# An encoder layer on one core: tokens in residue order, bias tables as one Toeplitz block per residue distance

## The chip, the cores and the metric

The kernel runs on one core of one Trainium2 chip. The metric is the device time of one execution in microseconds (us). TensorE is written PE, VectorE DVE, ScalarE ACT, GpSimd POOL, SyncE SP.

## What is computed

One encoder layer over two sequences, a prompt of 512 tokens and a sample of 256, model width 1024, all in float32. After an RMSNorm, one projection gives the queries, keys, values and gates of two attention branches: differential attention (4 heads, all keys) and dilated attention (3 groups of 4 heads). Their gated sum is projected back, and a mixture of 16 expert MLPs follows. A T5 table adds to each logit a bias that depends only on key position minus query position. The dilated branch, cut to what matters:

```python
DIL_CONFIGS = ((128, 1), (512, 4), (2048, 16))     # (window, dilation)
def dilated_group(q, k, v, bias_table, window, dilation):
    # Query i attends to i + m*dilation for |m*dilation| <= window/2 (keys gathered by stride).
    L = S // dilation
    def residues(t):
        return t.reshape(B, L, dilation, H, dh).transpose(0, 2, 1, 3, 4)
    ...
    off = jnp.arange(KW)[None, :] - W - jnp.arange(Q_BLOCK)[:, None]
    band = jnp.abs(off) <= W
    bias = bias_table[t5_bucket(off * dilation)].transpose(2, 0, 1)
    s = jnp.einsum('bmnqhd,bmnkhd->bmnhqk', qr, kblk) * scale + bias
    s = jnp.where(mask, s, NEG_INF)
    ...
# alpha = softmax of the three groups' log-denominators; ob = sum(alpha * outs)
```

## The kernel before

The 768 tokens are 6 tiles of 128: 4 of the prompt (`TP`), 2 of the sample. `ht_hi` and `ht_lo` hold the normed tokens turned round (model dimension on partitions, tokens in their order along the row), split in two float32r parts, so that each float32 product is three matmuls (`passes`, lines 777 to 779).

PE's order is written out by hand. It goes through 46 *halves* (`HALVES`), each a 128-column or 3-tile piece of the projection, and in fixed *slots* beside them it does the attention: one *unit* is (branch, head, tile), and `SCORES_IN` puts two units into a slot. In a slot PE turns the probabilities of the two units before (L835), forms the scores of two new ones (L815 differential, L823 and L825 dilated), does the half, and then multiplies probabilities by values (L857). A head's six units are its four prompt tiles and then its two sample tiles. Halves 0 to 3 are the differential values, 4 to 11 differential queries and keys, 12 to 17 the dilated values (two halves for each group g = 0, 1, 2), 18 to 29 the dilated queries and keys, 30 to 45 the gates. Differential scores stand in slots 9 to 20, dilated ones in slots 26 to 37.

Dilated attention needs the tokens of one residue (mod 4 in the prompt, mod 2 in the sample). `tile_columns` and `query_columns` pick them out of token order with a step: every 4th float32 column for prompt tiles, every 2nd for sample tiles. Three matmuls use this. The dilated values of groups 1 and 2 (halves 14 to 17) read `ht_hi` and `ht_lo` so as the stationary operand. Dilated scores read the queries so as the stationary operand; in the two far groups (L825) they read the keys so too, as the moving operand. One half's three tiles are 3 x 24 matmuls; the first half of a group holds prompt tiles 0 to 2, the second prompt tile 3 and both sample tiles.

The bias tables are made at the start: a one-hot matmul (`vectors`, L769, in slots 1 to 3) expands the table into vectors of length `VEC` = 3072 for 16 heads, ACT copies them out (`copy_vectors`) and stores them to DRAM, and POOL's `load_bias` reads skewed rows of them back. There are 8 loads, one per head and branch, into two buffers (`n % 2`). A load waits on `s_max` until every unit of the load two before it has been through `add_bias` on DVE (L1380 differential, L1388 and L1389 dilated).

Of the kernel before, what the change touches and what calls it, by code (L numbers as in the profile page):

```python
# [24 lines left out]
F32 = mybir.dt.float32  # L25
# [7 lines left out]
P = 128  # L33
# [26 lines left out]
SEC_DIFF, SEC_NEAR, SEC_D4, SEC_D16, SEC_SAMPLE_D4, SEC_SAMPLE_D16 = 0, 1024, 2048, 2304, 2560, 2816  # L60
# [93 lines left out]
VEC_SLOTS = 1  # L154
SUB_SLOT = {22: [0, 1], 23: [2, 3]}
# [27 lines left out]
BIAS_DMAS = [1] * H + [6] * H  # L183
# [18 lines left out]
def build(nc, x_prompt, x_sample, rel_bias, norm_mix, w_in, lam_q1, lam_k1, lam_q2, lam_k2, subln_g,  # L202
# [9 lines left out]
    with ctx:  # L212
# [31 lines left out]
        BIAS_W = 516 + 256 + 258 + 258  # L244
# [24 lines left out]
        junk = at("junk", [P, D], F32, A_ATT + 28800)  # L269
# [168 lines left out]

        def rows_of(t):
            return (x_prompt[0, P * t:P * t + P, :] if t < TP  # L440
                    else x_sample[0, P * (t - TP):P * (t - TP) + P, :])

        def out_rows(t):
            return (y_prompt[0, P * t:P * t + P, :] if t < TP
                    else y_sample[0, P * (t - TP):P * (t - TP) + P, :])
# [167 lines left out]
        def _(gp):  # L613
# [7 lines left out]
            def load_bias(n):  # L621

                if n >= 2:

                    gp.wait_ge(s_max, NT * (n - 1))
                b = bias[:, n % 2, :]
                done = s_bias[n % 2]
                if n < H:  # L630
                    gp.dma_start(b[:, 0:896], bass.AP(vec, n * VEC + SEC_DIFF, [[1, P], [1, 896]])).then_inc(done, 16)
                    return
                h = n - H
                r0 = (4 + h) * VEC + SEC_NEAR
                r1 = (8 + h) * VEC + SEC_D4
                r2 = (12 + h) * VEC + SEC_D16
                r3 = (8 + h) * VEC + SEC_SAMPLE_D4
                r4 = (12 + h) * VEC + SEC_SAMPLE_D16
                gp.dma_start(b[:, 0:516], bass.AP(vec, r0, [[4, P], [1, 516]])).then_inc(done, 16)
                gp.dma_start(b[:, 772:1029], bass.AP(vec, r0 + 256, [[2, P], [1, 257]])).then_inc(done, 16)  # L640
                for at0, r in ((516, r1), (516 + P, r2), (1030, r3), (1030 + P, r4)):
                    gp.dma_start(b[:, at0:at0 + P], bass.AP(vec, r, [[1, P], [1, P]])).then_inc(done, 16)

            gp.wait_ge(s_vec_out, 16)
            for n in range(2 * H):
                load_bias(n)
# [79 lines left out]
        def _(pe):  # L726
# [55 lines left out]
            def half(s):  # L782
                c, j = divmod(s, 2)
                if j == 0:
                    pe.wait_ge(s_wlo, c + 1)
                kind = HALVES[s][0]
                ps = main_item("half", s)
                hi, lo = e8(w_hi[:, c % 2, :]), e8(w_lo[:, c % 2, :])
                if kind in ("q", "k", "gate"):
                    cols = slice(P * j, P * j + P)  # L790
                    for a, b in ((0, 512), (512, T)):
                        last = passes(ps[:, a:b], [((hi[:, k, cols], lo[:, k, cols]),
                                                    (ht_hi[:, k, a:b], ht_lo[:, k, a:b])) for k in range(KD)])
                else:
                    res = kind == "vl" and HALVES[s][1] > 0
                    for i in range(3):
                        t = 3 * j + i
                        if s < 2:
                            pe.wait_ge(s_work_v, t + 1)
                        last = passes(ps[:, 256 * i:256 * i + 256],  # L800
                                      [((tile_columns(ht_hi[:, k, :], t, res), tile_columns(ht_lo[:, k, :], t, res)),
                                        (hi[:, k, :], lo[:, k, :])) for k in range(KD)])
                        if s < 2 and t + 2 < NT:
                            turn_x(t + 2)
                last.then_inc(s_main, 1)

            def score(u):
# [3 lines left out]
                if not dil:  # L811
                    for c in range(2):
                        rows = slice(HD * c, HD * c + HD)
                        at0 = c * 512
                        last = pe.matmul(ps[:, at0:at0 + S], query_columns(blk[rows, DIFF_Q[h], :], t, False),  # L815
                                         blk[rows, DIFF_K[h], s0:s0 + S], start=True, stop=True)
                else:
                    rows = slice(HD * (h % 2), HD * (h % 2) + HD)
                    for g in range(N_DIL):
                        q = query_columns(blk[rows, DIL_Q[h // 2][g], :], t, True)  # L820
                        k = blk[rows, DIL_K[h // 2][g], :]
                        if g == 0:
                            last = pe.matmul(ps[:, 0:S], q, k[:, s0:s0 + S], start=True, stop=True)  # L823
                        else:
                            last = pe.matmul(ps[:, 384 + P * g:512 + P * g], q, tile_columns(k, t, True),  # L825
                                             start=True, stop=True)
# [43 lines left out]
            for s in range(N_SLOTS):  # L870
# [8 lines left out]
                if VEC_SLOTS <= s < VEC_SLOTS + 3:  # L879
# [175 lines left out]
        def _(act):  # L1055
# [36 lines left out]
            def copy_vectors(i):  # L1092
                ps = work_ready("vec", i)
                act.activation(vecs[:, 1024 * i:1024 * i + 1024], ps[0:16, :], ACT.Copy).then_inc(s_work_a, 1)
                if i == 2:

                    act.wait_ge(s_work_a, emptied(WORK, WORK_NO[("vec", 2)], WORK_BY_VECTOR)[1])
# [25 lines left out]
            def empty_pv(u):  # L1123
# [6 lines left out]
                act.activation(tile_columns(ob[rows, h // 2, :], t, True)[:, ::-1], ps[rows, 0:P], ACT.Copy).then_inc(s_work_a, 1)  # L1130
# [19 lines left out]
            for s in range(N_SLOTS):  # L1150
# [9 lines left out]
                if VEC_SLOTS <= s < VEC_SLOTS + 3:  # L1160
                    copy_vectors(s - VEC_SLOTS)
                if s == VEC_SLOTS + 3:
# [158 lines left out]
        def _(dve):  # L1321
# [44 lines left out]
            def add_bias(u):  # L1366

                dil, h, t = UNITS[u]
                n = H * dil + h
                _, S = sequence(t)  # L1370
# [3 lines left out]
                if t == 0:  # L1374
                    dve.wait_ge(s_bias[n % 2], bias_count(n))
                dve.wait_ge(s_work, WORK_NO[("score", u)] + 1)
                if not dil:
                    at0 = 384 - P * (t if t < TP else t - TP)
                    for c in range(2):
                        last = dve.tensor_tensor_reduce(prob[:, i, 512 * c:512 * c + S], ps[:, 512 * c:512 * c + S],  # L1380
                                                        b[:, at0:at0 + S], 1.0, LOWEST, ALU.add, ALU.max, mx[:, i, c:c + 1])
# [4 lines left out]
                near = b[:, 3 - t:3 - t + S] if t < TP else b[:, 773 - (t - TP):773 - (t - TP) + S]  # L1386
                far = b[:, 516:772] if t < TP else b[:, 1030:1286]
# [32 lines left out]
            for s in range(N_SLOTS):  # L1420
# [6 lines left out]
                if s == VEC_SLOTS + 4:  # L1427
# [305 lines left out]
def _onehot(np):  # L1733
# [8 lines left out]
    rel = np.arange(-511, 513)  # L1742
    put(SEC_DIFF, rel, rel > 511)
    put(SEC_NEAR, rel, np.abs(rel) > 64)
# [35 lines left out]
```

## Time and profile before

| | us |
|---|---|
| median of 3 runs | 1008.6 |
| lowest, highest | 1008.04, 1009.04 |
| profiled execution, span from first to last instruction | 1006.1 |
| PE busy | 894.9 (89%) |
| DVE busy | 470.4 (47%) |
| ACT busy | 395.8 (39%) |
| POOL busy | 186.7 (19%) |

Of the profiled execution the span is shown, 2.5 us under the median of the runs. Busy shares are means over stages with different limits. Matmuls overlap their neighbours, so the start of one matmul to the start of the next tells what it costs, and its own duration does not.

### The profile page before, as it was taken

What the parts mean: (1) busy time and instruction counts of PE and PEld (TensorE: products, weight loads), DVE (VectorE), ACT (ScalarE), POOL (GpSimd) and SP (SyncE); (2) the same over time, 40 slices, a digit from 0 to 9 for tenths busy, and PEclk for the clock granted to TensorE, in tenths of its full rate; (3) what the DMA queues carried; (4) which work ended last, traced back from release to release, by engine and by line L of the source; (5) the groups of instructions that cost most, each with busy time, mean ns of one, the idle gap of its engine ahead of it and who ended that gap; (6) DMA issues with size and microseconds to landing.
All of it is one profiled execution on the core that took longest, in us unless ns stands there. A gap on an engine that the chain in (4) does not pass through costs nothing.

```text
span 1006.1 us, 13215 instructions
## 1 busy us (share of the span) xinstructions
PE 894.9 (89%) x5004; PEld 768.8 (76%) x5004; DVE 470.4 (47%) x754; ACT 395.8 (39%) x534; POOL 186.7 (19%) x124
## 2 busy tenths in 40 slices
PE   4999999999999999999999999999814999899920
PEld 4988788998788888888888888888613788788810
DVE  4411544333519523132322126622484688768638
ACT  5432444233433433324333211211530677677614
POOL 0000000001010010100000000400051476768644
PEclk9999999999999998999999999999955999999975
DMA  9231210112130321111102121691692699998775
GB/s 295 74 97 43 84 52 18 54 42 52 26 94 8 84 69 42 27 42 43 43 19 66 43 83 43 208 401 48 252 333 70 216 386 379 377 330 299 239 273 228
DMA packets 96397, 140.41 MB, mean 140 GB/s; under 512 B 4283, under 2 KB 75147, under 8 KB 96299
## 3 DMA queue, kind: packets, MB, share of 16 engines
q1 hardware_dynamic: 89276, 114.91, 33.8%
q0 software_dynamic: 7040, 24.61, 7.6%
q8 instruction: 35, 0.57, 0.2%
q10 hardware_dynamic: 32, 0.20, 0.2%
q14 instruction: 14, 0.11, 0.0%
HBM read 114.34 MB, written 25.36 MB: 139 GB/s over the span
## 4 chain that ended last, share of the span: by engine, by line
PE 78%; DVE 9%; DMA 4%; ACT 4%; issue 2%; SPq 2%; POOL 1%; ACTq 0%; POOLq 0%; DVEq 0%
PE main L777 20%; PE main L778 20%; PE main L779 20%; PE work L857 4%; PE work L823 2%; PE work L815 2%; PE work L825 2%; PE work L997 2%; DMA xg<-h_rows,column 1%; PE work L835 1%; ACT prob_t L1121 1%; DVE x L1715 1%; DMA e_raw<-in_w_exp_down 1%; DVE w_lo L1332 1%; PE work L950 1%
## 5 line engine op out<-in xcount | busy, mean ns | idle before, releaser
L777 PE MATMUL main<-ht_hi,w_hi 128*128 128x512 f32 (+1 forms) x576 | 198.5, 345 | 0.0
L778 PE MATMUL main<-ht_lo,w_hi 128*128 128x512 f32 (+1 forms) x576 | 195.6, 340 | 0.0
L779 PE MATMUL main<-ht_hi,w_lo 128*128 128x512 f32 (+1 forms) x576 | 195.2, 339 | 0.0
L1332 DVE TENSOR_TENSOR w_lo<-raw,w_hi 128x2048 fp32r<-128x2048 f32 x30 | 68.7, 2290 | 265.7 <-ACT w_hi L1065 265.7
L777 PEld LDWEIGHTS main<-ht_hi,w_hi 128*128 128x128 f32 x576 | 110.3, 192 | 19.0 <-issue 6.4
L779 PEld LDWEIGHTS main<-ht_hi,w_lo 128*128 128x128 f32 x576 | 110.2, 191 | 12.2
L778 PEld LDWEIGHTS main<-ht_lo,w_hi 128*128 128x128 f32 x576 | 110.4, 192 | 11.9
L777 PE MATMUL main<-w_hi,ht_hi 128*128 128x256 f32 (+1 forms) x304 | 102.4, 337 | 3.4 <-DVE ht_lo L1349 3.4
L778 PE MATMUL main<-w_lo,ht_hi 128*128 128x256 f32 (+1 forms) x304 | 100.8, 332 | 0.0
L779 PE MATMUL main<-w_hi,ht_lo 128*128 128x256 f32 (+1 forms) x304 | 100.7, 331 | 0.0
L1213 ACT ACTIVATE e_hi<-e_raw 128x2048 fp32r<-128x2048 f32 x48 | 90.5, 1910 | 15.2 <-DMA e_raw<-in_w_exp_down 6.8
L1511 DVE TENSOR_TENSOR e_lo<-e_raw,e_hi 128x2048 fp32r<-128x2048 f32 x31 | 71.5, 2337 | 21.4 <-ACT e_hi L1213 21.3
L777 PEld LDWEIGHTS main<-w_hi,ht_hi 128*128 128x128 f32 x304 | 67.8, 223 | 11.7 <-issue 8.5
L778 PEld LDWEIGHTS main<-w_lo,ht_hi 128*128 128x128 f32 x304 | 67.9, 223 | 2.5
L779 PEld LDWEIGHTS main<-w_hi,ht_lo 128*128 128x128 f32 x304 | 67.8, 223 | 2.5
L1065 ACT ACTIVATE w_hi<-raw 128x2048 fp32r<-128x2048 f32 x30 | 57.2, 1907 | 25.9 <-PE main L779 24.3
L685 POOL TENSOR_TENSOR e_lo<-e_raw,e_hi 128x2048 fp32r<-128x2048 f32 x13 | 61.6, 4740 | 25.5 <-ACT e_hi L1213 25.5
L777 PE MATMUL main<-e_hi,xt_hi 128*128 128x512 f32 x152 | 61.9, 407 | 0.0
L779 PE MATMUL main<-e_hi,xt_lo 128*128 128x512 f32 x152 | 60.1, 396 | 0.0
L778 PE MATMUL main<-e_lo,xt_hi 128*128 128x512 f32 x152 | 60.1, 395 | 0.0
L1142 ACT ACTIVATE blk<-main 128x768 f32<-128x768 f32 x16 | 13.0, 811 | 94.7 <-PE main L779 94.7
L1380 DVE CUSTOM_DVE_ANT_0 prob<-work,bias 128x512 f32<-128x512 f32 (+1 forms) x48 | 26.9, 598 | 39.6 <-PE work L815 39.6
(237 smaller groups left out, 1522.9 us busy)
## 6 DMA issues: line engine op xcount, KB each, us to landing
e_raw<-in_w_exp_gate SPq DMA_DIRECT2D x16, 1024.0 KB, 8.9
e_raw<-in_w_exp_up SPq DMA_DIRECT2D x16, 1024.0 KB, 9.7
e_raw<-in_w_exp_down SPq DMA_DIRECT2D x16, 1024.0 KB, 9.3
raw<-in_w_in SPq DMA_DIRECT2D x28, 512.0 KB, 5.1
expert_rows<-y_sb SPq DMA_DIRECT2D x19, 512.0 KB, 8.4
raw<-in_w_in SPq DMA_DIRECT2D x9, 1024.0 KB, 5.6
expert_rows<-y_sb SPq DMA_DIRECT2D x1, 5632.0 KB, 22.6
raw<-in_w_out SPq DMA_DIRECT2D x4, 1024.0 KB, 5.7
```

What stands on the lines that cost most here:

```text
L685: gp.tensor_tensor(lo, e_raw[j % 2][:, c, :], hi, ALU.subtract).then_inc(s_elo[c], 1)
L777: pe.matmul(out, s_hi, m_hi, start=(first and i == 0), stop=False)
L778: pe.matmul(out, s_hi, m_lo, start=False, stop=False)
L779: last = pe.matmul(out, s_lo, m_hi, start=False, stop=(final and i == n - 1))
L815: last = pe.matmul(ps[:, at0:at0 + S], query_columns(blk[rows, DIFF_Q[h], :], t, False), blk[rows, DIFF_K[h], s0:s0 + S], start=True, stop ...
L823: last = pe.matmul(ps[:, 0:S], q, k[:, s0:s0 + S], start=True, stop=True)
L857: last = pe.matmul(ps[:, 0:P], v, prob_t[:, u % 2, P * i:P * i + P], start=(i == 0), stop=(i == n - 1))
L1065: act.activation(w_hi[:, c % 2, :], raw[:, c % 2, :], ACT.Copy).then_inc(s_whi, 1)
L1213: act.activation(e_hi[:, par, c, :], e_raw[par][:, c, :], ACT.Copy).then_inc(s_ehi[c], 1)
L1332: dve.tensor_tensor(w_lo[:, c % 2, :], raw[:, c % 2, :], w_hi[:, c % 2, :], ALU.subtract).then_inc(s_wlo, 1)
L1380: last = dve.tensor_tensor_reduce(prob[:, i, 512 * c:512 * c + S], ps[:, 512 * c:512 * c + S], b[:, at0:at0 + S], 1.0, LOWEST, ALU.add, AL ...
L1511: dve.tensor_tensor(e_lo[:, par, c, :], e_raw[par][:, c, :], e_hi[:, par, c, :], ALU.subtract).then_inc(s_elo[c], 1)
```

## The change

Tile t of the prompt now holds the tokens 4p + t and tile t of the sample the tokens 2p + t, from the load of x to the store of y: partition p of a tile is a row 4 (or 2) rows further on in DRAM. A residue's tokens then lie side by side, and `tile_columns` and `query_columns` are plain slices in both branches. Keys that are neighbours in a tile are 4 (or 2) apart in position, so the bias of a query tile against a key tile is one 128 x 128 Toeplitz block that depends on the difference of the two residues: `2k - 1` blocks for `k` tiles. Prompt and sample need different blocks, so there are 16 loads (head and sequence) in place of 8, and `VEC` is 4096 in place of 3072, which makes four one-hot parts of three.

```diff
-SEC_DIFF, SEC_NEAR, SEC_D4, SEC_D16, SEC_SAMPLE_D4, SEC_SAMPLE_D16 = 0, 1024, 2048, 2304, 2560, 2816
+SEC_DIFF, SEC_SAMPLE_DIFF, SEC_NEAR, SEC_SAMPLE_NEAR = 0, 1024, 1536, 2560
+SEC_D4, SEC_D16, SEC_SAMPLE_D4, SEC_SAMPLE_D16 = 3072, 3328, 3584, 3840
 VEC = SEC_SAMPLE_D16 + 256
...
-def tile_columns(block, t, residues):
-    if not residues:
-        return block[:, P * t:P * t + P]
-    if t < TP:
-        return block[:, t:S_PROMPT:4]
-    return block[:, S_PROMPT + t - TP:T:2]
+def tile_columns(block, t):
+    return block[:, P * t:P * t + P]
...
-def query_columns(block, t, residues):
-    if not residues:
-        return block[:, P * (NT - 1 - t):P * (NT - t)]
-    if t < TP:
-        return block[:, T - 4 * P + 3 - t:T:4]
-    return block[:, 1 - (t - TP):S_SAMPLE:2]
+def query_columns(block, t):
+    return block[:, P * (NT - 1 - t):P * (NT - t)]
...
+VEC_PARTS = VEC // 1024
-    WORK += [("vec", i) for i in range(3) if s == VEC_SLOTS + i]
+    WORK += [("vec", i) for i in range(VEC_PARTS) if s == VEC_SLOTS + i]
...
-BIAS_DMAS = [1] * H + [6] * H
+BIAS_DMAS = [2, 2] * H + [3, 3] * H
+def units_before(n):
+    return NT * (n // 2) + UNITS_OF[0] * (n % 2)
...
+        xp_v, yp_v = (a[0].rearrange("(p r) d -> r p d", r=TP) for a in (x_prompt, y_prompt))
+        xs_v, ys_v = (a[0].rearrange("(p r) d -> r p d", r=NT - TP) for a in (x_sample, y_sample))
         def rows_of(t):
-            return (x_prompt[0, P * t:P * t + P, :] if t < TP
-                    else x_sample[0, P * (t - TP):P * (t - TP) + P, :])
+            return xp_v[t] if t < TP else xs_v[t - TP]
...
             def load_bias(n):
                 if n >= 2:
-                    gp.wait_ge(s_max, NT * (n - 1))
+                    gp.wait_ge(s_max, units_before(n - 1))
...
+                head, short = divmod(n, 2)
+                dil, h = divmod(head, H)
+                k = NT - TP if short else TP
+                row = (4 * dil + h) * VEC
+                first = row + ((SEC_DIFF, SEC_NEAR), (SEC_SAMPLE_DIFF, SEC_SAMPLE_NEAR))[short][dil]
+                gp.dma_start(b[:, 0:k * P].rearrange("p (r j) -> p r j", r=k),
+                             bass.AP(vec, first, [[1, P], [256, k], [1, P]])).then_inc(done, 16)
+                gp.dma_start(b[:, k * P:(2 * k - 1) * P].rearrange("p (r j) -> p r j", r=k - 1),
+                             bass.AP(vec, first + 1, [[1, P], [256, k - 1], [1, P]])).then_inc(done, 16)
+                if dil:
+                    far = (8 + h) * VEC + (SEC_SAMPLE_D4 if short else SEC_D4)
...
             def add_bias(u):
-                n = H * dil + h
+                n = 2 * (H * dil + h) + (t >= TP)
+                r, k = (t, TP) if t < TP else (t - TP, NT - TP)
+                near = b[:, (k - 1 - r) * P:(k - 1 - r) * P + S]
-                if t == 0:
+                if r == 0:
                     dve.wait_ge(s_bias[n % 2], bias_count(n))
```

Most matmuls stand where they stood; what differs in them is the step of an operand. Two things move. On POOL, the bias loads near the start of the program stood so before (one load per differential head, then a near prompt table, a near sample table and four far blocks per dilated head):

```order
L631 DMA bias<-bias_vectors 128x896 x4
L639 DMA bias<-bias_vectors 128x516
L640 DMA bias<-bias_vectors 128x257
L642 DMA bias<-bias_vectors 128x128 x4
L639 DMA bias<-bias_vectors 128x516
```

and they stand so after the change, where the first eight rows are two differential heads, prompt and then sample:

```order
L634 DMA bias<-bias_vectors 128x4x128
L636 DMA bias<-bias_vectors 128x3x128
L634 DMA bias<-bias_vectors 128x2x128
L636 DMA bias<-bias_vectors 128x128
L634 DMA bias<-bias_vectors 128x4x128
L636 DMA bias<-bias_vectors 128x3x128
L634 DMA bias<-bias_vectors 128x2x128
L636 DMA bias<-bias_vectors 128x128
```

Each differential head has four DMAs in pieces of 128 floats where it had one in rows of 896, and each dilated head six as before (three for each sequence). On PE, after the half of slot 4, the program before goes straight to the half of slot 5:

```order
L777 MATMUL main0<-ht_hi_49,w_hi_52 128x256
L778 MATMUL main0<-ht_lo_50,w_hi_52 128x256
L779 MATMUL main0<-ht_hi_49,w_lo_53 128x256
L777 MATMUL main1<-ht_hi_49,w_hi_52 128x512 [waits s_main_a]
L778 MATMUL main1<-ht_lo_50,w_hi_52 128x512
```

and the changed one does the fourth one-hot part in between:

```order
L777 MATMUL main0<-ht_hi_49,w_hi_52 128x256
L778 MATMUL main0<-ht_lo_50,w_hi_52 128x256
L779 MATMUL main0<-ht_hi_49,w_lo_53 128x256
L769 MATMUL work1<-onehot_64,table_66 16x512 [waits s_work_a]
L769 MATMUL work1<-onehot_64,table_66 16x512
L777 MATMUL main1<-ht_hi_49,w_hi_52 128x512 [waits s_main_a]
```

Two matmuls have come in between, and with them ACT's copy of the fourth part; the store of the vectors to DRAM moves behind that copy.

## Rows read from the trace of the kernel before

**Rows 1.** Page, part 1: busy us (share of the span) and instructions by engine.

```profile
PE 894.9 (89%) x5004; PEld 768.8 (76%) x5004; DVE 470.4 (47%) x754; ACT 395.8 (39%) x534; POOL 186.7 (19%) x124
```

**Rows 2.** Windows, halves 12, 14 and 15; the sum is over halves 12 to 17.

```profile
core 0: us, PE busy (x) PEld busy (x) DVE busy (x) ACT busy (x) POOL busy (x), PEclk, DMA share, GB/s
144.20:152.93 8.73, 8.73 (x74) 8.73 (x73) 7.87 (x19) 3.31 (x9) 0.00 (x0) 1.00 0.45 122
...
170.44:187.36 16.92, 16.92 (x75) 16.92 (x74) 6.23 (x19) 3.20 (x9) 0.54 (x1) 1.00 0.31 89
192.01:203.47 11.46, 11.46 (x74) 11.46 (x73) 5.25 (x18) 2.94 (x8) 0.00 (x0) 1.00 0.00 1
...
sum 74.22, PE 74.22 PEld 74.21 DVE 36.16 ACT 17.72 POOL 3.71; mean PE 12.37 PEld 12.37 DVE 6.03 ACT 2.95 POOL 0.62
```

**Rows 3.** Timeline of PE in half 15, prompt tile 3 to sample tile 4.

```profile
start us, us, engine line op out<-in xcount [idle before <-releaser]
...
197.49 0.39 PE L779 MATMUL main<-w_hi,ht_lo 128*128 128x256 f32 x1
197.72 0.28 PE L777 MATMUL main<-w_hi,ht_hi 128*128 128x256 f32 x1
197.84 0.28 PE L778 MATMUL main<-w_lo,ht_hi 128*128 128x256 f32 x1
```

**Rows 4.** Timeline of PE, dilated scores of two prompt units and what follows.

```profile
344.01 1.25 PE L823 MATMUL work<-blk 64*128 64x512 f32 x2 [0.29 <-ACT prob_t L1121]
...
346.01 1.04 PE L823 MATMUL work<-blk 64*128 64x512 f32 x2
346.90 1.08 PE L825 MATMUL work<-blk 64*128 64x128 f32 x4
347.90 0.50 PE L777 MATMUL main<-ht_hi,w_hi 128*128 128x512 f32 x1
```

**Rows 5.** Timeline of PE, dilated scores of two sample units and what follows.

```profile
360.75 0.70 PE L823 MATMUL work<-blk 64*128 64x256 f32 x2 [0.19 <-ACT prob_t L1121]
...
361.76 0.59 PE L823 MATMUL work<-blk 64*128 64x256 f32 x2
362.20 0.63 PE L825 MATMUL work<-blk 64*128 64x128 f32 x4
362.75 0.50 PE L777 MATMUL main<-ht_hi,w_hi 128*128 128x512 f32 x1
```

**Rows 6.** Windows, halves after dilated prompt scores; columns as in rows 2.

```profile
333.78:342.25 8.47, 8.47 (x50) 7.49 (x49) 4.97 (x15) 2.19 (x5) 0.00 (x0) 1.00 0.47 126
379.05:389.09 10.04, 10.04 (x49) 8.62 (x49) 2.67 (x9) 1.76 (x4) 0.00 (x0) 0.83 0.00 0
...
sum 38.02, PE 38.02 PEld 33.05 DVE 14.95 ACT 7.65 POOL 0.00; mean PE 9.51 PEld 8.26 DVE 3.74 ACT 1.91 POOL 0.00
```

**Rows 7.** Timeline of PE, one-hot part of slot 1.

```profile
39.44 1.89 PE L769 MATMUL work<-onehot,table 33*16 33x512 f32 x4
41.25 0.39 PE L777 MATMUL main<-w_hi,ht_hi 128*128 128x256 f32 x1
```

**Rows 8.** Tile bias: durations ns min/median/max, first and last start us; landings.

```profile
L1380 DVE CUSTOM_DVE_ANT_0 prob<-work,bias x48: 416/684/694, 105.8 to 275.5; 128x512 f32<-128x512 f32 x32, 128x256 f32<-128x256 f32 x16
...
L631 POOL DMA_DIRECT2D bias<-bias_vectors x4: 537/558/724, 67.2 to 176.0; - x4
...
DMA to landing us min/median/max: 3.0/3.8/6.0
```

**Rows 9.** DMA issues: name, engine, count, size of each, median us to landing.

```profile
x_in<-in_x_prompt SPq DMA_DIRECT2D x4, 512.0 KB, 7.7
...
bias<-bias_vectors POOLq DMA_DIRECT2D x4, 448.0 KB, 4.6
...
w_rt<-in_w_router POOLq DMA_DIRECT2D x4, 16.0 KB, 2.8
```

**Rows 10.** Timeline of DVE: last prompt unit of head 0, first of head 1.

```profile
123.66 0.17 DVE L1384 TENSOR_SCALAR nmx<-mx 128x2 f32<-128x2 f32 x1
...
146.82 0.68 DVE L1380 CUSTOM_DVE_ANT_0 prob<-work,bias 128x512 f32<-128x512 f32 x1
```

More of the change, by code:

```diff
@@ L625, in load_bias @@
                 if n >= 2:
-                    gp.wait_ge(s_max, NT * (n - 1))
+                    gp.wait_ge(s_max, units_before(n - 1))
                 b = bias[:, n % 2, :]
                 done = s_bias[n % 2]
[L630 to L642, printed above, removed]
+                head, short = divmod(n, 2)
[9 more added lines that the diff above has]
+                    far = (8 + h) * VEC + (SEC_SAMPLE_D4 if short else SEC_D4)
+                    at0 = (2 * k - 1) * P
+                    gp.dma_start(b[:, at0:at0 + 2 * P].rearrange("p (g j) -> p g j", g=2),
+                                 bass.AP(vec, far, [[1, P], [4 * VEC + 256, 2], [1, P]])).then_inc(done, 16)
             gp.wait_ge(s_vec_out, 16)
-            for n in range(2 * H):
+            for n in range(4 * H):
                 load_bias(n)
@@ L794, in half @@
                 else:
-                    res = kind == "vl" and HALVES[s][1] > 0
                     for i in range(3):
@@ L814, in score @@
                         at0 = c * 512
-                        last = pe.matmul(ps[:, at0:at0 + S], query_columns(blk[rows, DIFF_Q[h], :], t, False),
+                        last = pe.matmul(ps[:, at0:at0 + S], query_columns(blk[rows, DIFF_Q[h], :], t),
                                          blk[rows, DIFF_K[h], s0:s0 + S], start=True, stop=True)
@@ L819, in score @@
                     for g in range(N_DIL):
-                        q = query_columns(blk[rows, DIL_Q[h // 2][g], :], t, True)
+                        q = query_columns(blk[rows, DIL_Q[h // 2][g], :], t)
                         k = blk[rows, DIL_K[h // 2][g], :]
@@ L824, in score @@
                         else:
-                            last = pe.matmul(ps[:, 384 + P * g:512 + P * g], q, tile_columns(k, t, True),
+                            last = pe.matmul(ps[:, 384 + P * g:512 + P * g], q, tile_columns(k, t),
                                              start=True, stop=True)
@@ L1129, in empty_pv @@
                 rows = slice(HD * (h % 2), HD * (h % 2) + HD)
-                act.activation(tile_columns(ob[rows, h // 2, :], t, True)[:, ::-1], ps[rows, 0:P], ACT.Copy).then_inc(s_work_a, 1)
+                act.activation(tile_columns(ob[rows, h // 2, :], t)[:, ::-1], ps[rows, 0:P], ACT.Copy).then_inc(s_work_a, 1)
             def empty_half(s):
@@ L1377, in add_bias @@
                 if not dil:
-                    at0 = 384 - P * (t if t < TP else t - TP)
                     for c in range(2):
                         last = dve.tensor_tensor_reduce(prob[:, i, 512 * c:512 * c + S], ps[:, 512 * c:512 * c + S],
-                                                        b[:, at0:at0 + S], 1.0, LOWEST, ALU.add, ALU.max, mx[:, i, c:c + 1])
+                                                        near, 1.0, LOWEST, ALU.add, ALU.max, mx[:, i, c:c + 1])
                     last.then_inc(s_work_v, 1)
@@ L1385, in add_bias @@
                     return
-                near = b[:, 3 - t:3 - t + S] if t < TP else b[:, 773 - (t - TP):773 - (t - TP) + S]
-                far = b[:, 516:772] if t < TP else b[:, 1030:1286]
+                far = b[:, (2 * k - 1) * P:(2 * k + 1) * P]
                 dve.tensor_tensor_reduce(prob[:, i, 0:S], ps[:, 0:S], near, 1.0, LOWEST, ALU.add, ALU.max, mx[:, i, 0:1])
@@ L1740, in put @@
         hot[row, cols] = 1.0
-    rel = np.arange(-511, 513)
-    put(SEC_DIFF, rel, rel > 511)
-    put(SEC_NEAR, rel, np.abs(rel) > 64)
+    for k, at_diff, at_near in ((TP, SEC_DIFF, SEC_NEAR), (NT - TP, SEC_SAMPLE_DIFF, SEC_SAMPLE_NEAR)):
+        rel = (k * np.arange(256)[None, :] + np.arange(k)[:, None] - (k * P - 1)).reshape(-1)
+        put(at_diff, rel, rel >= k * P)
+        put(at_near, rel, np.abs(rel) > 64)
     off = np.arange(-127, 129)
```

25 lines of the change are left out of this document (13 added, 12 removed).

## The prediction

> **What bounds the kernel now.** I read the page's busy shares first: PE is busy 894.9 of the 1006.1 us span, DVE and ACT under half of it [rows 1]. So I looked for stretches in which PE itself is slow, not for waits. The windows over the halves 12 to 17 (the dilated values) show one. All six halves are 72 matmuls of the same shape, and PE is busy throughout each, at full clock. Half 12 takes 8.73 us; half 14 takes 16.92 and half 15 takes 11.46 [rows 2]. Halves 12 and 13 read their tokens side by side. Half 14 reads three prompt tiles with a step of four floats, half 15 one prompt tile so and two sample tiles with a step of two. The timeline inside half 15 separates the two steps: with step 4 a matmul starts 0.23 us after the one before it (197.49 to 197.72), and from the first matmul with step 2 it is 0.12 us (197.72 to 197.84) [rows 3]. That is 8.73 / 72 = 0.121, the pace of half 12. So a step of two floats costs nothing here and a step of four costs a factor of 1.9. The reader is to see that only prompt tiles are slow, and that no other engine ends a wait there.
>
> The dilated scores show the same. Two prompt units take 347.90 - 344.01 = 3.89 us [rows 4], two sample units 362.75 - 360.75 = 2.00 us [rows 5]. Their far parts (L825) have the same sizes, yet the second unit's, with the way into the next half, takes 1.00 us for the prompt (346.90 to 347.90) and 0.55 for the sample (362.20 to 362.75).
>
> **The change part by part.** All sums are made against the profiled span of 1006.1 us; the median of the runs is 2.5 us above it, and I carry that over.
>
> *Dilated values.* The stationary operand of halves 14 to 17 becomes a plain slice. I give each of the six halves the 8.73 us of half 12: the sum of 74.22 [rows 2] - 6 x 8.73 = **21.8 us less**, all on PE. What must keep up is DVE and ACT, which lose the longer slots. Half 12 already ran at the short length with DVE busy 7.87 and ACT 3.31 of its 8.73 us and PE busy without a break, and it is the kind of slot that 14 to 17 become. So I take no new wait.
>
> The Trainium skill, SBUF — State Buffer (section "Door 1: The DMA port swizzle"), says that at least two accesses per 16-byte line are needed for full bandwidth, and then that a step of up to 4 fp32 is free. The first sentence agrees with rows 3, the second, read literally, does not; by it this term would be zero. The rows decide, and the reading is among the rivals.
>
> *Dilated scores.* There are 24 units, in 8 prompt pairs and 4 sample pairs. What a prompt pair costs with plain slices I build from the sample pair, whose step of two is free: its 2.00 us, plus the near group's extra columns. In the second unit, whose first weight load is hidden, near takes 362.20 - 361.76 = 0.44 us for 256 keys [rows 5]; 512 keys take twice that, and the prompt's own 346.90 - 346.01 = 0.89 [rows 4] confirms it. That makes 2.00 + 2 x 0.44 = 2.88 us, 1.01 less than 3.89, and over 8 pairs **8.1 us less**. Bounds: 0.7 per pair if only the moving keys gain and the queries' loads do not, 1.2 if the break of 0.29 us ahead of the scores closes to the sample's 0.19 too.
>
> *Clock.* After three of the eight prompt pairs the half that follows ran partly at 1.2 GHz: that at 379.05 took 10.04 us at a mean granted clock of 0.83, against 8.47 at 1.00 for an undisturbed one [rows 6]. The three together lost 38.02 - 4 x 8.47 = 4.1 us. PE had no idle time in these halves; what stood just before each was 3.9 us of slow, 64-row score matmuls. No sample pair (2.0 us) and no differential pair was followed by such a drop. With 2.9 us of denser matmuls I expect the drops to go: **4.1 us less**, bounds 0 and 4.1.
>
> The Trainium skill, TensorE: Matmul & The Clock Gate (section "HAM oscillation — how this bites in real kernels"), asks only for the absence of idle gaps between bursts. By that, drops without a gap have another cause and would stay, and the sum would be 4.1 us worse; this too is a rival.
>
> *Fourth one-hot part.* Two matmuls of L769 stand after half 4 with nothing to hide them on PE. The part in slot 1 took 41.25 - 39.44 = 1.81 us from its first matmul to the next half [rows 7]: **1.8 us more**. ACT's copy lies beside the next half. The store of the vectors moves back by about one half and one part, some 10 us. The first bias load was issued at 67.2 and its first use was at 105.8 [rows 8]; issued at about 78 and with the longest bias landing of 6.0 us it is there 20 us early. Without that cover all of the delay would show, once.
>
> *Bias loads.* POOL waits on DVE's row maxima, and behind a waiting load stand only later loads and, far later, the reload of x, for which nobody waits in the attention. But the lead shrinks. A head's prompt blocks can be fetched when the previous head's prompt units are done, and are needed two slots later: 146.82 - 123.66 = 23.2 us in the differential stage [rows 10], before which it was a whole head. The sample's have three slots. A prompt load is 2 or 3 DMAs in pieces of 512 bytes, 896 pieces in the differential stage instead of 128. No row has this shape. Below: bias landings were 3.0 to 6.0 us whatever the row length [rows 8], and 1024 pieces of 16 bytes landed in 2.8 us [rows 9]. Above: if time went with the number of pieces, 4.6 us for 448 KB [rows 9] would become 7 x 4.6 = 32 us. I take some 8 us (issues included), nearest to the row with 1024 pieces: hidden, 0.
>
> *Rows of x and y.* The same 4 KB row goes to each partition, only 4 or 2 rows apart in DRAM. Loads of x took 7.7 us to land in the crowded start [rows 9]; below, no change; above, at half the pace, 7.7 us late at the start, when PE waits for the first tiles. The last stores would add less. I take 0, because the pieces keep their size. The larger one-hot table (a third more) has until 39.44 [rows 7] to land; 0. DVE's adds and all other matmuls keep their shapes.
>
> **Sum.** -21.8 - 8.1 - 4.1 + 1.8 = -32.2 us: span 973.9, and at the median 1008.6 - 32.2 = **976.4 us**, about 3.2% faster.
>
> **Rivals.**
>
> 1. *The clock still drops* after about as many prompt pairs: 976.4 + 4.1 = 980.5 us. For it: no idle time precedes the drops. Against: only the longest score stretches had them.
> 2. *Strided rows in DRAM slow the start*: up to 976.4 + 7.7 = 984 us. For it: x is what the start waits for. Against: unchanged piece size.
> 3. *The step is not what is slow*, so that the change doesn't do what it says: 1008.6 + 1.8 = 1010.4 us. Rows 3 speak plainly against it: the pace changes inside one half, between two matmuls of the same line and shape.
> 4. *Slower: bias blocks come late.* The place is DVE's first add of each new head, where PE's scores pile up in two PSUM buffers. Prompt loads 2, 4, 6, 10, 12 and 14 have the short lead. At 32 us against 23.2 each is 9 us late: 6 x 9 = 54, 976 + 54 = 1030 us. It ends slower than before from about 6 us of lateness per load, a load of 29 us. The 2.8 us for 1024 pieces speaks against it.
> 5. *The short slots bind another engine* and half of the 21.8 us is lost: 987 us. Against: half 12.
>
> **How the numbers follow.** Forecast 0.66, rival 1 0.14, rival 2 0.08, rival 3 0.03, rival 4 0.04, rival 5 0.05. The range goes from 971 (all upper bounds: 8 x 0.2 = 1.6 from the scores, and some 4 us if breaks such as 0.29 us ahead of the scores close in 12 slots or the clock rises earlier elsewhere) to 983, which takes in the clock rival and a mild form of the second. Faster by over 0.2% (2 us, about what a measurement of this kernel can tell from no change) 0.93, within 0.2% 0.03 (rival 3), slower 0.04 (rival 4).
>
> **What would show it.** Halves 14 to 17 at about 8.7 us each, with 0.12 us between matmuls; prompt score pairs at about 2.9 us; the halves behind them all at about 8.5 us and full clock; a fourth L769 group of 1.8 us; no wait of DVE for a bias DMA; PE's start on the first tile unchanged. It is wrong if DVE waits for bias at the heads' first units, if ACT or DVE ends PE's waits in slots 14 to 17, or if the pace stays at 0.23 us with plain slices.

## The result, and the profile after

The changed kernel takes 978.6 us (median of 4 runs, 976.1 to 980.7); the kernel before, run beside it on the same chip, takes 1008.8 us (4 runs). The ratio is 0.968, with a 95% interval of 0.966 to 0.970. The forecast was 976.4 us, in a range of 971 to 983. A second measurement of the same kernel is told below as the run "again". The profiled execution took 977.4 us, of which 975.6 are the span. Lines that stood behind the changed code have other numbers now: the dilated scores are L822 and L824 (before L823 and L825).

Page, part 1, of the changed kernel, to be read beside [rows 1]:

```profile
PE 862.5 (88%) x5008; PEld 732.6 (75%) x5008; DVE 472.1 (48%) x754; ACT 394.6 (40%) x535; POOL 198.6 (20%) x136
```

PE lost 32.4 us of busy time (894.9 to 862.5) although the trace has four more matmuls (it records two for each of the two new one-hot matmuls), and the span became 30.5 us shorter. DVE and ACT do what they did. So the time came out of work on PE, not out of waits, and a view of waits would not have shown where.

Windows over the dilated value halves 13 to 17, which answer to [rows 2]:

```profile
core 0: us, PE busy (x) PEld busy (x) DVE busy (x) ACT busy (x) POOL busy (x), PEclk, DMA share, GB/s
159.66:168.38 8.72, 8.72 (x74) 8.72 (x73) 5.37 (x16) 2.94 (x8) 1.48 (x2) 1.00 0.28 55
172.68:181.42 8.74, 8.74 (x75) 8.74 (x73) 6.30 (x19) 3.19 (x9) 1.26 (x2) 1.00 0.57 139
186.07:194.79 8.72, 8.72 (x74) 8.72 (x73) 5.25 (x18) 2.94 (x8) 0.00 (x0) 1.00 0.00 1
199.28:208.01 8.73, 8.73 (x74) 8.73 (x73) 7.92 (x19) 3.26 (x9) 1.48 (x2) 1.00 0.61 149
212.31:221.04 8.73, 8.73 (x74) 8.73 (x73) 3.73 (x18) 2.08 (x8) 1.26 (x2) 1.00 0.29 24
```

Half 14, the second row, went from 16.92 to 8.74 us, half 15 from 11.46 to 8.72. DVE has to do the same work in the shorter slots and fills up to 7.92 of 8.73 us, but PE is busy throughout each row: nothing else became the bound.

Timeline of PE over a pair of dilated prompt units, which answers to [rows 4], and windows over two halves that follow such pairs, which answer to [rows 6]:

```profile
323.26 1.12 PE L822 MATMUL work<-blk 64*128 64x512 f32 x2 [0.29 <-ACT prob_t L1120]
...
326.06 0.50 PE L777 MATMUL main<-ht_hi,w_hi 128*128 128x512 f32 x1
```

```profile
313.05:321.50 8.45, 8.45 (x50) 7.49 (x50) 6.03 (x15) 3.27 (x5) 0.00 (x0) 1.00 0.47 127
326.06:334.55 8.49, 8.49 (x49) 7.48 (x49) 2.99 (x10) 2.06 (x4) 2.22 (x3) 1.00 0.29 69
```

The pair takes 326.06 - 323.26 = 2.80 us (before 3.89). The break of 0.29 us ahead of it is still there. All eight halves behind such pairs run at a granted clock of 1.00, at 8.4 to 8.5 us; before, three of the eight did not.

Timeline of PE at the new fourth one-hot part, and DVE's first add of the second head, beside [rows 7] and [rows 10]:

```profile
71.36 1.89 PE L769 MATMUL work<-onehot,table 33*16 33x512 f32 x4
73.18 0.50 PE L777 MATMUL main<-ht_hi,w_hi 128*128 128x512 f32 x1
```

```profile
125.95 0.17 DVE L1384 TENSOR_SCALAR nmx<-mx 128x2 f32<-128x2 f32 x1
...
149.05 0.68 DVE L1380 CUSTOM_DVE_ANT_0 prob<-work,bias 128x512 f32<-128x512 f32 x1
```

The part costs 73.18 - 71.36 = 1.82 us. The time in which a head's bias has to arrive is 23.1 us. What a load needs of that stands in the view of the tile bias (operation, count, shortest, median and longest duration in ns, first and last start), beside [rows 8]:

```profile
L634 POOL DMA_DIRECT2D bias<-bias_vectors x16: 705/744/951, 78.5 to 435.4; - x16
...
  DVE nmx L1391: 165.7, 6
  DVE nmx L1384: 164.9, 8
  DMA bias_vectors<-vecs: 77.3, 1
  PE work L824: 44.5, 6
  PE work L814: 22.8, 6
...
DMA to landing us min/median/max: 3.5/4.0/4.7
```

The five indented rows tell for what the engines that use this tile sat idle, and how often: POOL for DVE's maxima and once for the store of the vectors, DVE for PE's scores (L814 and L824). No row says that DVE waited for a bias DMA. Landings take 3.5 to 4.7 us of the 23.1.

By stage: the last values matmul of the attention starts at 497.4 us, before at 530.3, which is 32.9 us less; the forecast's sum was 32.2. From there to the end it takes 478.2 us, before 475.8. Windows over these three stretches (PEclk is the third figure from the end of a row), first of the kernel before, then of the changed one:

```profile
530.30:704.00 173.70, 171.10 (x903) 147.22 (x902) 64.24 (x59) 37.74 (x35) 10.06 (x15) 1.00 0.35 125
704.00:780.00 76.00, 35.34 (x208) 28.38 (x207) 46.94 (x93) 26.00 (x31) 18.10 (x11) 0.69 0.63 220
780.00:1006.10 226.10, 175.82 (x847) 145.18 (x845) 161.76 (x154) 135.28 (x128) 142.90 (x62) 0.90 0.85 303
```

```profile
497.40:671.00 173.60, 171.02 (x903) 147.21 (x902) 64.21 (x59) 37.70 (x35) 10.16 (x15) 1.00 0.35 125
671.00:748.80 77.80, 36.87 (x207) 29.25 (x207) 46.93 (x93) 26.03 (x31) 18.12 (x11) 0.67 0.61 214
748.80:975.60 226.80, 175.93 (x848) 145.10 (x846) 161.79 (x154) 135.36 (x128) 141.40 (x62) 0.90 0.85 302
```

The change touches nothing of this work but the order of the tokens and the rows that x is read from again and y is stored to. The middle stretch, the router, is 1.8 us longer at a lower mean clock; the experts are 0.7 us longer at the same mean clock. The stores of y are not the reason: they land in 2.6 to 5.2 us before and 2.6 to 5.3 after, and from DVE's last instruction to the end it is 3.1 and 3.0 us. Whether the longer stretch belongs to the change is a question for the runs.

### The profile page after: what moved, and what is told of

It reads as the page before. It is cut to its first block, busy times and chain, and to the rows that moved or that the text cites. A ratio compares the mean times of both kernels' runs of the same rounds, so it can differ in the third digit from the quotient of the medians.

```text
span 975.6 us, 13244 instructions
## 1 busy us (share of the span) xinstructions
PE 862.5 (88%) x5008; PEld 732.6 (75%) x5008; DVE 472.1 (48%) x754; ACT 394.6 (40%) x535; POOL 198.6 (20%) x136
## 4 chain that ended last, share of the span: by engine, by line
PE 77%; DVE 9%; DMA 4%; ACT 4%; SPq 3%; issue 2%; POOL 1%; ACTq 0%; POOLq 0%; DVEq 0%
PE main L777 20%; PE main L778 19%; PE main L779 19%; PE work L856 4%; PE work L814 2%; PE work L822 2%; PE work L996 2%; DMA xg<-h_rows,column 1%; PE work L834 1%; ACT prob_t L1120 1%; DVE x L1714 1%; PE work L824 1%; PE work L949 1%; SPq L534 1%; DMA raw<-in_w_in 1%
## 5 line engine op out<-in xcount | busy, mean ns | idle before, releaser
L777 PE MATMUL main<-w_hi,ht_hi 128*128 128x256 f32 (+1 forms) x304 | 94.9, 312 | 3.5 <-DVE ht_lo L1348 3.5
L634 POOL DMA_DIRECT2D bias<-bias_vectors x16 | 12.0, 750 | 407.9 <-DVE nmx L1391 165.7
L778 PE MATMUL main<-w_lo,ht_hi 128*128 128x256 f32 (+1 forms) x304 | 93.4, 307 | 0.0
L779 PE MATMUL main<-w_hi,ht_lo 128*128 128x256 f32 (+1 forms) x304 | 93.3, 307 | 0.0
L777 PEld LDWEIGHTS main<-w_hi,ht_hi 128*128 128x128 f32 x304 | 58.6, 193 | 11.8 <-issue 8.5
L778 PEld LDWEIGHTS main<-w_lo,ht_hi 128*128 128x128 f32 x304 | 58.7, 193 | 2.5
L779 PEld LDWEIGHTS main<-w_hi,ht_lo 128*128 128x128 f32 x304 | 58.6, 193 | 2.5
```

The costliest lines, as they stand in the source:

```text
L777: pe.matmul(out, s_hi, m_hi, start=(first and i == 0), stop=False)
L778: pe.matmul(out, s_hi, m_lo, start=False, stop=False)
L779: last = pe.matmul(out, s_lo, m_hi, start=False, stop=(final and i == n - 1))
```

## The experiments

All kernels below are the changed one with one edit, except "again", which has none, and "before_b", which is the kernel before. Where a time is said to be of one execution, it is that of the profiled execution.

**again: the changed kernel once more.** No edit.

> The changed kernel as it is, once more. Theory: the attention (up to the end of the last probabilities-by-values matmul) ends about 33 us earlier than before in every execution, and what differs between executions is the granted clock in the router and at the start of the experts. Time 977 to 980 us. Rival: part of the attention's gain is itself a matter of the execution, so that the attention's end moves by some us from one profile to the next (495 to 500 us and more).

Measured: 977.0 us (median of 6 runs, 976.4 to 980.2), ratio 0.968 (0.965 to 0.970). The attention ends at 497.7 us, with no drop of the clock behind a prompt pair, and the rest takes 476.8 us. So the end of the attention repeats to a few tenths in the changed kernel, and what lies behind it moves by a microsecond or two. Over 13 profiles of the kernels of this study the rest takes 474.7 to 479.7 us; the two of the kernel before have 475.8 and 475.5, six of the changed kernel or of one that differs only in its loads have 474.7 to 478.2. The 2.4 us by which this stretch was longer in the first profile (478.2 against 475.8) lie within this spread. Sorted by the rows of x and y the spread says one thing more: the four profiles with rows side by side (the two of the kernel before, "rows_a" and "rows_b" below) have 474.7 to 475.8, the nine with rows apart 475.7 to 479.7. A cost of the change of a microsecond or two behind the attention is therefore not excluded; no run separates it, since "rows_a" and "rows_b" also compute other values.

**values: the dilated values read with the old steps, all else as changed.**

```
+ cols = slice(P * t, P * t + P)
+ if kind == "vl" and HALVES[s][1] > 0:
+     cols = slice(t, S_PROMPT, 4) if t < TP else slice(S_PROMPT + t - TP, T, 2)
- ((tile_columns(ht_hi[:, k, :], t), tile_columns(ht_lo[:, k, :], t)),
+ ((ht_hi[:, k, cols], ht_lo[:, k, cols]),
```

It picks the values of other tokens than it should; the amount of work is the same.

> Only the dilated values of groups 1 and 2 read ht_hi and ht_lo with the steps of four and two of the kernel before (they pick other tokens than the reference, since the tokens now lie in residue order). Theory: the step of the stationary operand is all of the first term, so halves 14 and 16 are back at 16.9 us, 15 and 17 at 11.5, and the time is 21.8 us above the changed kernel's: about 1000.4 us. Rival: the slow halves came from something else that the token order brought along; then the halves stay near 8.7 us and the time near 978.6.

Measured: 1000.5 us (median of 4 runs, 998.6 to 1001.4). This is 21.9 us over the changed kernel's first measurement and 23.5 over "again", which ran beside it on the same chip; by the profiles, which leave out what lies behind, the attention ends 22.0 us later than in "again" (519.7 against 497.7). Windows over halves 14 and 15 of this kernel:

```profile
173.10:190.02 16.92, 16.92 (x75) 16.92 (x74) 6.30 (x19) 3.19 (x9) 1.26 (x2) 1.00 0.33 74
194.66:206.12 11.46, 11.46 (x74) 11.46 (x73) 5.27 (x18) 2.93 (x8) 0.00 (x0) 1.00 0.00 1
```

These are the durations of [rows 2] to the hundredth. The step alone makes them, whatever else the change did. No half behind a prompt pair fell to a lower clock here: slow values do not bring the drops.

**both: the dilated scores read with the old steps, queries and keys, all else as changed.** Here and in "queries" and "keys", scores are taken between other tokens than the reference's.

```
- q = query_columns(blk[rows, DIL_Q[h // 2][g], :], t)
+ q = stepped_queries(blk[rows, DIL_Q[h // 2][g], :], t)   # block[:, T - 4 * P + 3 - t:T:4] for the prompt
- ... q, tile_columns(k, t),
+ ... q, stepped_keys(k, t),                               # block[:, t:S_PROMPT:4] for the prompt
```

> Only the dilated scores read queries and keys with the steps of the kernel before (other tokens than the reference's). Theory: prompt pairs are back at 3.9 us, 8 x 1.1 = 8.7 us more, and drops of the clock after some of them return, 1.4 us each, 3 as in the kernel before: 978.6 + 8.7 + 4.1 = 991.4 us. Rival on the clock: the drops have another cause than the slow scores and stay away: 987.3 us.

Measured: 990.4 us (median of 4 runs, 989.3 to 995.3), 11.8 us over the changed kernel's first measurement and 13.4 over "again". Prompt pairs take 3.89 us again, and behind three of the eight the clock fell; the window over one of these halves:

```profile
315.43:325.49 10.06, 10.06 (x49) 8.61 (x49) 4.96 (x15) 2.19 (x5) 0.00 (x0) 0.83 0.40 107
```

Pairs and drops came back together, with the values plain. So the drops belong to the scores' steps.

**steps: halves 12 to 17 of the values with steps 2, 3, 4, 5, 6 and 1.** It multiplies values of other tokens than it should; counts and shapes stay.

```
+ step = {12: 2, 13: 3, 14: 4, 15: 5, 16: 6}.get(s, 1)
+ first = 0 if kind == "vl" else P * t
+ cols = slice(first, first + P * step, step)
- ((tile_columns(ht_hi[:, k, :], t), tile_columns(ht_lo[:, k, :], t)),
+ ((ht_hi[:, k, cols], ht_lo[:, k, cols]),
```

> The six dilated value halves read the stationary operand with steps of 2, 3, 4, 5, 6 and 1 floats (halves 12 to 17 in this order; other tokens than the reference's). Theory, lines of 16 bytes: what counts is how many 16-byte lines 128 columns touch, up to one line a column at a step of four: 8.7 us at step 2, about 0.75 of 16.8 = 12.6 us at step 3, 16.8 us at 4, 5 and 6 alike, 8.7 us at 1. Rival, distance: the cost goes on growing with the step, some 21 us at 5 and 25 us at 6. Rival, powers of two: 4 alone is slow, 3, 5 and 6 near 8.7 us.

Measured: windows over the six halves, in order of the steps 2, 3, 4, 5, 6, 1 (one execution, 1007.7 us):

```profile
147.37:156.12 8.75, 8.75 (x74) 8.75 (x73) 7.89 (x19) 3.31 (x9) 0.00 (x0) 1.00 0.45 122
160.61:173.21 12.60, 12.60 (x75) 12.60 (x74) 5.37 (x16) 2.94 (x8) 1.48 (x2) 1.00 0.19 38
177.49:194.41 16.92, 16.92 (x74) 16.92 (x73) 6.30 (x19) 3.20 (x9) 1.26 (x2) 1.00 0.35 74
199.06:215.62 16.56, 16.56 (x75) 16.56 (x74) 5.25 (x18) 2.93 (x8) 0.00 (x0) 1.00 0.00 0
220.11:236.69 16.58, 16.58 (x75) 16.58 (x73) 8.31 (x19) 3.25 (x9) 1.48 (x2) 1.00 0.43 91
240.98:249.72 8.74, 8.74 (x75) 8.74 (x74) 3.75 (x18) 2.08 (x8) 1.26 (x2) 1.00 0.32 24
```

Step 2 is free, step 3 costs 3.9 us a half, and from step 4 on it is a flat 7.8 to 8.2. A cost that grew with the distance would have gone on rising at 5 and 6, and one that only powers of two bring would have left 3, 5 and 6 alone. What fits is how many floats a 16-byte line still gives to the read: at least two up to step 2, one from step 4 on, and a mix of both at step 3. Worked out: four columns at step 3 touch three such lines, so 0.75 of the 16.92 us of step 4 is 12.7, against 12.60 measured, and at steps 5 and 6 each column has a line of its own as at step 4. Two reads per line for the full pace is what the Trainium skill says in SBUF — State Buffer, section "Door 1: The DMA port swizzle" (at least two accesses per line for full bandwidth); its other sentence there, that a step of up to 4 fp32 is free, does not hold in these rows. Why 5 and 6 are 0.3 us below 4 is open.

**queries and keys: only one operand of the dilated scores with the old step.** In "queries" it is the stationary operand (first line of the edit of "both"), in "keys" the moving operand of the far groups (second line).

> Only the queries of the dilated scores (stationary) have the steps of the kernel before; keys are plain slices (other tokens than the reference's). Theory: a prompt pair's loss sits in the loading of the stationary operand, which a far matmul of 128 columns is too short to cover: prompt pairs 3.8 to 3.9 us, as with both. Rival: the moving keys cost as much; then about 3.3 us.

> Only the keys of the far groups (moving) have the steps of the kernel before; queries are plain slices (other tokens than the reference's). Theory: a far matmul in float32 streams slowly enough to take a step of four, prompt pairs 2.8 to 2.9 us and no drop of the clock after them. Rival: the moving operand is slowed as the stationary one is: 3.3 us or more.

Measured, one execution each: 990.5 us with only the queries stepped and 989.4 us with only the keys. Timeline of PE over the first prompt pair, queries and then keys:

```profile
312.97 1.25 PE L834 MATMUL work<-blk 64*128 64x512 f32 x2
...
316.74 0.50 PE L789 MATMUL main<-ht_hi,w_hi 128*128 128x512 f32 x1
```

```profile
311.28 1.12 PE L834 MATMUL work<-blk 64*128 64x512 f32 x2
...
315.01 0.50 PE L789 MATMUL main<-ht_hi,w_hi 128*128 128x512 f32 x1
```

A pair takes 316.74 - 312.97 = 3.77 us in the one and 315.01 - 311.28 = 3.73 us in the other, where both steps cost 3.89 and none 2.80. The view of the tile work shows the far groups' weight loads and matmuls (shortest, median and longest in ns); queries, keys (the line is L836 in these two), and the changed kernel, in this order:

```profile
L836 PEld LDWEIGHTS work<-blk x96: 192/306/328, 313.6 to 488.5; 64*128 64x128 f32 x96
L836 PE MATMUL work<-blk x96: 269/336/497, 314.1 to 488.6; 64*128 64x128 f32 x96
```

```profile
L836 PEld LDWEIGHTS work<-blk x96: 184/187/307, 311.8 to 489.3; 64*128 64x128 f32 x96
L836 PE MATMUL work<-blk x96: 270/394/403, 312.2 to 489.4; 64*128 64x128 f32 x96
```

```profile
L824 PEld LDWEIGHTS work<-blk x96: 187/188/188, 310.8 to 475.0; 64*128 64x128 f32 x96
L824 PE MATMUL work<-blk x96: 269/272/272, 311.2 to 475.1; 64*128 64x128 f32 x96
```

A stepped stationary operand lengthens its load from 188 to 306 ns and with it the matmuls' median to 336; a stepped moving operand leaves the load at 187 and lengthens the matmul from 272 to 394; with both steps the medians are 306 and 394. Either alone brings back nearly the whole cost, and the two do not add. The theory for "queries" was nearly met (3.77 us for 3.8 to 3.9), but its reason, that the loss sits in the stationary operand, was half of the matter. The theory for "keys", that this operand's step costs next to nothing and that the clock holds, fell on both counts: the pair is slow, and the clock fell behind four of eight pairs, at the same place of each head (in "queries" it fell behind two, and there within the pair already: the pair took 3.87 us at 0.95 and 0.89). One of the four in "keys":

```profile
328.94:339.00 10.06, 10.06 (x50) 8.62 (x49) 2.95 (x9) 1.66 (x4) 2.22 (x3) 0.83 0.26 59
```

That load and matmul run beside each other, so that the slower one sets the pace, is the reading that fits these durations; no run took it apart further.

**late_loads: each prompt bias load waits for two units more.** This takes from the lead that the loads had.

```
- gp.wait_ge(s_max, units_before(n - 1))
+ gp.wait_ge(s_max, min(units_before(n - 1) + 2 * ((n + 1) % 2), units_before(n)))
```

> Each load of prompt blocks waits for two units more, those of the sample, so that it is issued one slot before it is needed in place of two (lead about 14 us). Same result as the reference. Theory: a load takes 6 to 7 us with its issues, so nothing waits: the heads' first adds start as before, time 976 to 981 us. Rival (bias blocks come late): DVE waits for the DMA at the first add of heads 1 to 3 in each branch and PE behind it.

**pieces: the first DMA of each bias load cut in four, in pieces of 32 floats.**

```
- gp.dma_start(b[:, 0:k * P]..., bass.AP(vec, first, [[1, P], [256, k], [1, P]])).then_inc(done, 16)
+ for q in range(0, P, 32):
+     gp.dma_start(b[:, 0:k * P]...[:, :, q:q + 32], bass.AP(vec, first + q, [[1, P], [256, k], [1, 32]])).then_inc(done, 16)
```

> The first DMA of each bias load is cut into four, in pieces of 32 floats in place of 128: four times as many pieces, the same bytes. Same result as the reference. Theory: the landing hardly goes with the number of pieces; all is landed within 10 us of the wait's end, and nobody waits: 976 to 981 us. Rival: time goes with pieces, a load takes over 20 us, and DVE waits at the heads' first units: some us per head, 985 us and more.

Measured, one execution each: 977.9 us with later loads and 976.3 us with four times the pieces, both within the changed kernel's own 976.1 to 980.7. With later loads the second head's prompt blocks are issued from 135.5 us on and first used at 149.4, a lead of 13.9 us. DVE waits for no bias DMA in either run, and the heads keep their pace. Tile bias of "pieces", the loads and the landings:

```profile
L635 POOL DMA_DIRECT2D bias<-bias_vectors x64: 702/747/968, 79.9 to 439.4; - x64
...
DMA to landing us min/median/max: 2.7/3.2/4.7
```

64 DMAs in place of 16 cost POOL its time to issue (five of about 0.7 us for a differential load in place of two), and bias DMAs land in 2.7 to 4.7 us. Each of the 64 has as many pieces as the DMA that it is a quarter of, with a quarter of the bytes, so its landing alone does not tell the price of a piece; that the whole load, with most of its pieces cut in four, makes nobody wait does. The plainer comparison is with the kernel before: 128 rows of 3.5 KB had a median landing of 4.6 us [rows 9], and the changed kernel's DMAs, of up to 512 pieces of 512 bytes, land in 3.5 to 4.7 us. So the time did not go with the number of pieces, the forecast's upper bound of 32 us for a load was far off, and rival 4 is out.

**rows_a and rows_b: the rows of x and y from and to DRAM side by side again.** Here the tokens stand in another order than the attention takes them for. rows_b is the same kernel once more.

```
- xp_v, yp_v = (a[0].rearrange("(p r) d -> r p d", r=TP) for a in (x_prompt, y_prompt))
+ xp_v, yp_v = (a[0].rearrange("(r p) d -> r p d", r=TP) for a in (x_prompt, y_prompt))
  (and the same for xs_v, ys_v)
```

> The changed kernel with tiles of 128 consecutive rows loaded from x and stored to y as before, so that only the distance of a tile's rows in DRAM is undone (the tokens are then no longer in residue order, and the dilated branch and the biases belong to other tokens than the reference's). Theory: rows 16 KB apart land later; the first tile lands about 1 us sooner here, PE starts at 8.4 us as in the kernel before and not at 8.9 to 10.1 as in the eight profiles of changed kernels so far, and slot 4 starts at about 62.5. Rival: the start moves from one execution to the next whatever the rows, and this profile lies among the others.

> The same kernel a second time, for the spread of the start between executions. Theory and rival as for the first.

Measured: 975.3 and 976.0 us, one execution each. The shortest landing of a tile of x, which is the first tile's, counted from its issue at 0.8 us, in the view of the tile x_in, in rows_a and in the changed kernel:

```profile
DMA to landing us min/median/max: 3.4/10.7/11.1
```

```profile
DMA to landing us min/median/max: 4.8/9.9/11.0
```

With rows side by side the first tile is there at 4.1 to 4.3 us of the span in all four profiles that read them so (the two of the kernel before among them), with rows apart at 4.8 to 5.5 us in all nine. So rival 2 has a true core: the first tile comes 0.5 us later at least and 1.4 at most. But this does not visibly reach the work behind. PE's first matmul, which the theory put at 8.4 us, starts at 9.3 and 9.7 in rows_a and rows_b, and at 8.9 to 10.1 with rows apart. The first one-hot part starts at 40.8 and 41.1 us in rows_a and rows_b, at 39.7 and 40.0 in the two profiles of the changed kernel, and elsewhere at up to 42.3. My theory for these runs, that PE and slot 4 start at about the same early time whenever the first tile is early, fell; the start moves by more than that from execution to execution.

**before_b: the kernel before once more, one execution.**

> The kernel before, as it is, a second time. Theory: the start as in its first profile, first matmul at 8.4 and first tile landed 3.5 us after its issue, and drops of the clock after some of the prompt pairs (two to four of eight). From the end of the attention to the end of the program 475.6 to 479.6 us, the spread of the profiles so far. Rival: the start moves here as well, to 9 us or more.

Measured: 1006.4 us; the first tile lands 3.4 us after its issue, but PE's first matmul starts at 9.0 us, as the rival had it. The attention ends at 529.1 us and the rest takes 475.5. Only one of eight halves behind a prompt pair fell to the lower clock, fewer than the two to four of the theory:

```profile
443.70:453.39 9.69, 9.69 (x49) 8.40 (x49) 2.67 (x9) 1.64 (x4) 0.00 (x0) 0.86 0.00 0
```

The first profile of the kernel before had three, so the clock term is a matter of one execution. Counted from the start of the first one-hot part to the last values matmul, the kernel before takes 490.9 us in its first profile and 488.2 here; the changed kernel takes 457.8 both times.

## Why the prediction was right, point by point

- **Dilated values:** forecast 21.8 us less. The six halves take 8.72 to 8.74 us each, 52.4 against 74.2, which is 21.8 less; "values", which undoes this alone, moves the end of the attention by 22.0 us. The step of half 15 that was read between two neighbouring matmuls was the whole cause. Of the Trainium skill's two sentences the one that agreed with [rows 3] holds also for steps 3, 5 and 6. Rivals 3 and 5 are out.
- **Dilated scores:** forecast 2.88 us per prompt pair, 8.1 us less in all; measured 2.80, so 8 x 1.09 = 8.7 less. The term is mis-sized by 0.6 us: the estimate took the sample pair's step of two as free, but with plain slices that pair too went from 2.00 to 1.95 us (340.90 - 338.95 in its timeline), and each unit's 256 keys more take (2.80 - 1.95) / 2 = 0.43 us and not 0.44. The lower bound of the gain was wrong in its reasoning: it let the moving keys gain alone and priced that at 0.7 us a pair. By "queries" and "keys" a gain in one operand alone is worth 0.12 to 0.16 us a pair (3.89 to 3.77 or 3.73); only both together bring 1.09.
- **Clock:** forecast 4.1 us less, and all drops went. Over the 13 profiles, 13 of 40 prompt pairs with a stepped operand were followed by a drop, and 0 of 64 with plain ones. The term was sized from a profile with three drops; other profiles of stepped scores had one to four, at 1.1 to 1.6 us each, so that it is worth some 1.2 to 5.7 us from execution to execution. That the drops go with the steps was read rightly; that their size of 4.1 us also fitted is luck in part, since it was taken from one profile and set against that same profile. What sets off a drop was not taken apart further. The halves themselves have no idle time, and the break of 0.29 us ahead of a pair stays where the drops went. The Trainium skill's rule (TensorE: Matmul & The Clock Gate, section "HAM oscillation — how this bites in real kernels"), which asks only that there be no idle gaps between bursts, does not account for them. Rival 1 is out.
- **Fourth one-hot part:** forecast 1.8 us more, measured 1.82.
- **Bias loads:** forecast 0, right. The estimate of 8 us for a load was somewhat too high (landings of 3.5 to 4.7 us, and two or three issues of 0.7 us), and the two runs show that nobody waits with 13.9 us of lead in place of 23.1 either, nor with more pieces.
- **Rows of x and y:** forecast 0 for the whole, and PE's start unchanged. The first tile does land 0.5 to 1.4 us later, and PE's first matmul did not start unchanged (8.4 us before, 9.7 after), but it is at 9.0 in the second profile of the kernel before and at 9.3 and 9.7 with rows side by side again: what the rows do to the start is lost in its spread.
- **Sum:** -21.8 - 8.7 - 4.1 + 1.8 = -32.8 us, against 32.9 measured at the end of the attention and a forecast of 32.2. The median of the whole came out 30.2 us lower in the first measurement and 33.1 in the second (977.0 against 1010.1). The closeness of the sum holds for these two profiles: against the second profile of the kernel before, with one drop, the stretch from the first one-hot part to the attention's end gained 30.4 us and not 33.1. The 2.2 us by which the first measurement missed the forecast of 976.4 match the 2.4 us behind the attention, where the router ran longer at a lower clock; this stretch moves by some microseconds from profile to profile, and whether the change has a part in it is open ("again").

## What to carry to other kernels

When two stretches with the same matmuls take different times and PE is busy throughout both, compare the time from one matmul's start to the next inside one stretch, and look at the step of its operands: reading fp32 with a step of 4 floats halved PE's pace here while the page showed PE merely as busy. Put the data in the order in which it is read, and do it for the stationary and the moving operand alike, since one slow operand kept nearly the whole cost of these short score matmuls. The order can often be had at the load from DRAM, whose price at the start was a first tile 0.5 to 1.4 us later; and a term that rests on the clock of one profile should be sized from several.

## What the runs showed of the hardware that was not expected

- A step of 3 floats is slower by 12.60 / 8.74 = 1.44, and steps 5 and 6 (16.56 and 16.58 us) are not slower than 4 (16.92).
- A stepped stationary operand slows its load (188 to 306 ns) and a stepped moving one its matmul (272 to 394 ns), and together they cost hardly more than either (3.89 against 3.77 and 3.73 us a pair).
- Pairs of slow 64-row score matmuls, with no idle gap between them and the next half, were followed by a granted clock of 0.83 to 0.87 over that half in 13 of 40 cases; halves of slow 128-row matmuls (16.92 us in "values" and "steps") kept 1.00.
- Bias DMAs in pieces of 512 bytes landed in 3.5 to 5.1 us (the changed kernel and "late_loads"), those of a quarter of the bytes in pieces of 128 bytes in 2.7 to 4.0 ("pieces").
